# The first block of a two-block network: where the panel casts and low parts stand in the order of ScalarE and VectorE

## The reference

```
proj = rmsnorm(h) @ w_in                      # 4376 columns
hq, hf, hi, hgo, hz, nq, kcm, vcm, ksl, vsl, kwn, vwn, ngate, nz = split(proj)
o_hg = hgrn2_chunkwise(hq, log_f(hf), k(hf), hi)      # gated linear recurrence, 4 heads
y_hg = rmsnorm(o_hg) * sigmoid(hgo) * silu(hz)
kc, vc = compress(kcm), compress(vcm)         # overlapping blocks of 32 tokens, MLP with silu
o_cmp = softmax(q . kc) @ vc                  # compressed keys
o_slc, o_win = attention(q, k_sl, v_sl), attention(q, k_wn, v_wn)   # rope on q and k
y_nsa = (g0 * o_cmp + g1 * o_slc + g2 * o_win) * silu(nz)
h = h + concat(y_hg, y_nsa) @ w_out
h = h + sigmoid(rmsnorm(h) @ w_pg) * (p @ w_pp)
```

## Time and profile before

| | |
|---|---|
| median of 3 runs | 1097.96 us |
| the profiled execution: its own time | 1098.19 us |
| its span | 1096.3 us |
| busy TensorE, VectorE, ScalarE | 1030.5, 730.3, 599.5 us |
| granted clock of TensorE, mean | 0.979 |

### The profile page before, as it was taken

One profiled execution on the slowest core, in us unless ns is written; L12 is line 12 of the kernel. 1 busy time (PEld: TensorE's weight loads), 2 busy tenths in 40 slices (PEclk: granted clock), 3 DMA queues, 4 the chain that ended last, 5 costly groups with the idle time before them and its releaser, 6 DMA issues.

```text
span 1096.3 us, 21297 instructions
## 1 busy us (share of the span) xinstructions
PE 1030.5 (94%) x8933; PEld 971.7 (89%) x8933; DVE 730.3 (67%) x1101; ACT 599.5 (55%) x874; POOL 4.9 (0%) x13
## 2 busy tenths in 40 slices
PE   5999789899999888999999999999999999999997
PEld 4998677799996876998999999999888899999997
DVE  6855556578647455689677766666866588667664
ACT  5643565467536455577746654455655466545552
POOL 1000000000000000000000000000000000000000
PEclk8999899999999899999999999999999999999998
DMA  9453622155645321284543655555455245555531
GB/s 289 143 160 90 195 77 78 39 172 175 188 128 170 101 78 39 77 269 136 181 156 117 230 180 173 184 191 182 117 183 164 77 154 193 189 172 178 189 116 39
DMA packets 144747, 163.57 MB, mean 149 GB/s; under 512 B 6072, under 2 KB 135552, under 8 KB 144672
## 3 DMA queue, kind: packets, MB, share of 16 engines
q1 hardware_dynamic: 143752, 161.04, 45.9%
q10 hardware_dynamic: 632, 1.30, 0.3%
q0 software_dynamic: 288, 0.14, 0.1%
HBM read 161.43 MB, written 1.05 MB: 148 GB/s over the span
## 4 chain that ended last, share of the span: by engine, by line
PE 70%; DVE 12%; ACT 9%; issue 4%; DMA 3%; SPq 0%; ACTq 0%; DVEq 0%
PE ps L441 21%; PE ps L442 21%; PE ps L443 20%; ACT panels_high L1193 4%; DVE panels_low L1735 4%; DMA panels<-in_w_in 3%; ACT probs L1179 2%; PE ps L459 2%; DVE neg_max L1758 1%; DVE squares L1699 1%; DVE probs L1774 1%; DVE input_low L1695 1%; PE ps L664 1%; PE ps L543 1%; PE ps L599 0%
## 5 line engine op out<-in xcount | busy, mean ns | idle before, releaser
L1735 DVE TENSOR_TENSOR panels_low<-panels,panels_high 128x2048 fp32r<-128x2048 f32 (+1 forms) x146 | 330.0, 2263 | 227.8 <-ACT panels_high L1193 227.0
L441 PE MATMUL ps<-input_high,panels_low 128*128 128x256 f32 x1600 | 462.3, 289 | 17.6 <-DVE input_low L1730 7.5
L442 PE MATMUL ps<-input_low,panels_high 128*128 128x256 f32 x1600 | 454.7, 284 | 0.0
L443 PE MATMUL ps<-input_high,panels_high 128*128 128x256 f32 x1600 | 454.4, 284 | 0.0
L1193 ACT CAST panels_high<-panels 128x2048 fp32r<-128x2048 f32 (+1 forms) x146 | 274.3, 1880 | 151.9 <-PE ps L443 122.4
L441 PEld LDWEIGHTS ps<-input_high,panels_low 128*128 128x128 f32 x1600 | 308.8, 193 | 25.5 <-issue 8.1
L442 PEld LDWEIGHTS ps<-input_low,panels_high 128*128 128x128 f32 x1600 | 309.1, 193 | 0.1
L443 PEld LDWEIGHTS ps<-input_high,panels_high 128*128 128x128 f32 x1600 | 308.9, 193 | 0.0
L441 PE MATMUL ps<-ffn_hidden_high,panels_low 128*128 128x256 f32 x352 | 99.2, 282 | 3.1 <-issue 2.9
L442 PE MATMUL ps<-ffn_hidden_low,panels_high 128*128 128x256 f32 x352 | 99.6, 283 | 0.0
L443 PE MATMUL ps<-ffn_hidden_high,panels_high 128*128 128x256 f32 x352 | 99.4, 282 | 0.0
(11 more groups left out here) (288 smaller groups left out, 1309.3 us busy)
## 6 DMA issues: line engine op xcount, KB each, us to landing
panels<-in_ffn_up SPq DMA_DIRECT2D x44, 1024.0 KB, 5.1
panels<-in_w_in SPq DMA_DIRECT2D x32, 1024.0 KB, 6.0
panels<-in_ffn_down SPq DMA_DIRECT2D x22, 1024.0 KB, 4.9
panels<-in_mix_w_in SPq DMA_DIRECT2D x20, 1024.0 KB, 5.5
panels<-in_w_out SPq DMA_DIRECT2D x8, 1024.0 KB, 5.1
panels<-in_w_pg SPq DMA_DIRECT2D x8, 1024.0 KB, 5.7
panels<-in_mix_w_out SPq DMA_DIRECT2D x8, 1024.0 KB, 5.1
panels<-in_w_pp SPq DMA_DIRECT2D x2, 1024.0 KB, 4.8
```

The lines of the kernel that those rows point to most:

```text
L441: pe.matmul(dst, w[1], x[0], start=start, stop=False if not kw else True, **kw)
L442: pe.matmul(dst, w[0], x[1], start=False, stop=False if not kw else True, **kw)
L443: return pe.matmul(dst, w[0], x[0], start=False, stop=stop, **kw)
L1735: V.tensor_tensor(low_slots[slot][:, 0:size], raw[n % SLOTS][:, 0:size], high_slots[slot][:, 0:size].bitcast(F32), ALU.subtract).then_inc( ...
```

## The change

Four things move; no computation is added or left out.

- TensorE: level (7,1) is issued ahead of the rotated keys' product, and so ahead of the compressed keys.
- ScalarE: from `hidden_parts` to the copy of qr1 no casts; up to `cmp_kv` casts only of panels ahead of hz1. From the first `scores` to `on` casts only behind turned copies. The load of the table with exp and tanh moves from behind the output norm to behind the copy of hz0. The third quarter of the mixed rows' high part moves from `on` to `mixed`.
- VectorE: from `hidden_parts` to `cmp_kv` no low parts, but hgo1's at the entry of hgo0's copy. From the first `scores` to `on` low parts only behind row maxima. Row maximum 0 stands ahead of the output norm. The third quarter of the mixed rows' low part stands in the second `nsa_gate`.

```diff
@@ -781,6 +781,7 @@
                     todo(("copy", f"qr{j}"))
                 some(1)
                 gate_chunk()
+                some(16)
                 pe.wait_ge(k_rope_ready, l + 1)
                 begin(f"kr_{l}", 4)
                 pe.matmul(ps[4][:, :], ident, UK[:, 0:512], start=True, stop=False)
@@ -791,7 +792,6 @@
                 product(f"kc_{l}", 5, 32, W2[:, 0:P], HID[:, 0:32])
                 product(f"vc_{l}", 3, 64, HIDV[:, :], W2[:, P:P + 64])
                 todo(("cmp_kv",))
-                some(16)
                 gate_chunk()
                 pe.wait_ge(kcsq_ready, l + 1)
                 product(f"kcss_{l}", 5, 32, head_ones, KC[:, 32:64])
@@ -1335,11 +1335,13 @@
                         "vs": VT[:, 0:T], "ct": PCT[:, :], "hgo0": SG[:, 0:512], "hgo1": SG[:, 512:1024],
                         "hz0": HZ[:, 0:512], "hz1": HZ[:, 512:1024], "nz0": NZ[:, 0:512], "nz1": NZ[:, 512:1024]}
                 tanh_dest = {"hz0": FG[:, 0:512], "hz1": FG[:, 512:1024], "nz0": VH[:, 0:512], "nz1": VH[:, 512:1024]}
-                held = False
+                in_units = held = parts_out = kv_in = False
                 for place, step, *arg in agenda[l]:
                     if step == "copy" and arg[0] in tanh_dest:
                         name = f"{arg[0]}_{l}"
                         copy_out(name, dest[arg[0]], bank(name)[:, :])
+                        if arg[0] == "hz0":
+                            nc.scalar.preload_act_table_set(EXP_TANH)
                         drained(act, name)
                         f(tanh_dest[arg[0]], dest[arg[0]], ACT.Tanh, scale=0.5).then_inc(gate_tanh_ready, 1)
                     elif step == "copy":
@@ -1411,7 +1413,6 @@
                     elif step == "o_norm":
                         act.wait_ge(rope_ready, l + 1)
                         head_rinv([f"oss{g}_{l}" for g in range(2)], UK[:, :], P, 1024).then_inc(o_rinv_ready, 1)
-                        nc.scalar.preload_act_table_set(EXP_TANH)
                     elif step == "cmp_softmax":
                         act.wait_ge(cmp_shift_ready, l + 1)
                         f(SC[:, :], SC[:, :], ACT.Exp).then_inc(cmp_exp_ready, 1)
@@ -1425,13 +1426,16 @@
                         f(SG[:, :], SG[:, :], ACT.Tanh, scale=0.5).then_inc(sig_ready, 1)
                     elif step == "mixed":
                         full(act, f"nz1_{l}")
-                        mixed_high(l, None, (0, 1))
+                        mixed_high(l, [f"on0_{l}"], (0, 1, 2))
                     elif step == "on":
-                        mixed_high(l, [f"on{g}_{l}" for g in range(2)], (2, 3))
-
+                        mixed_high(l, [f"on{g}_{l}" for g in range(2)], (3,))
+
+                    in_units = (in_units or step == "scores") and step != "on"
                     held = (held or (step, *arg) == ("copy", "nz1")) and step != "on"
-                    if not held:
-                        split_high(place)
+                    parts_out = (parts_out or step == "hidden_parts") and (step, *arg) != ("copy", "qr1")
+                    kv_in = kv_in or step == "cmp_kv"
+                    if not held and not parts_out and (not in_units or step == "turned"):
+                        split_high(place, len(SPLIT_KEYS) if kv_in else SPLIT_NO[("hz1", l)])
 
                 squares(nidx, lambda g: drained(act, f"wo_{l}_{g}"), lambda g: split_after(f"wo_{l}_{g}") if g < 2 else None)
                 split_after(f"wo_{l}_2")
@@ -1947,6 +1951,7 @@
                 for g in range(2):
                     split_after(f"hq{g}_{l}")
                 split_after(f"hi{NT - 1}_{l}")
+                in_units = parts_out = False
                 for place, kind, *arg in agenda[l]:
                     if kind == "level":
                         level(*arg)
@@ -2015,6 +2020,7 @@
                                                          ALU.mult, ALU.mult)
                         ins.then_inc(kc_ready, 1)
                     elif kind == "o_norm":
+                        row_max(f"n{l}", 0, 8 * l)
                         dve.wait_ge(o_rinv_ready, l + 1)
                         step(V.scalar_tensor_tensor(QP[:, :], QP[:, :], vec("hgrn_onorm_g", l), UK[:, :],
                                                     ALU.mult, ALU.mult))
@@ -2045,7 +2051,7 @@
                                              r2.rearrange("p (n h) -> p n h", n=NT), gates[:, :, 0:8], ALU.mult))
                         V.tensor_tensor(s3, s3, r2.unsqueeze(2).to_broadcast([P, 16, 16]),
                                         ALU.mult).then_inc(cp_ready, 1)
-                    elif kind == "scores":
+                    elif kind == "scores" and arg[0] > 0:
                         row_max(f"n{l}", arg[0], 8 * l + arg[0])
                     elif kind == "normalise":
                         u = arg[0]
@@ -2069,6 +2075,8 @@
                         s = slice(arg[0] * 512, (arg[0] + 1) * 512)
                         dve.wait_ge(gate_tanh_ready, 4 * l + arg[0] + 3)
                         link(V.scalar_tensor_tensor(NZ[:, s], VH[:, s], 1.0, NZ[:, s], ALU.add, ALU.mult))
+                        if arg[0] == 1:
+                            mixed_low(l, 2)
                     elif kind == "mixed":
                         mixed_low(l, 0)
                         mixed_low(l, 1)
@@ -2077,9 +2085,12 @@
                         full(dve, name)
                         V.scalar_tensor_tensor(Y[:, 1536:2048], bank(name)[:, :], 0.5, NZ[:, 512:1024],
                                                ALU.mult, ALU.mult).then_inc(free(name), 1)
-                        mixed_low(l, 2)
                         mixed_low(l, 3)
-                    if kind not in ("level", "k_pad"):
+                    parts_out = (parts_out or kind == "hidden_parts") and kind != "cmp_kv"
+                    in_units = (in_units or kind == "scores") and kind != "on"
+                    if (kind, *arg) == ("copy", "hgo0"):
+                        split_low(place, SPLIT_NO[("hgo1", l)] + 1)
+                    elif kind not in ("level", "k_pad") and not parts_out and (not in_units or kind == "scores"):
                         split_low(place)
 
                 add_out(f"wo_{l}_", "", 2 * l + 1)
```

## The result

The changed kernel takes 1059.38 us (median of 4 runs, 1058.83 to 1059.88) against 1098.03 of the kernel before: ratio 0.965, 95% interval 0.9636 to 0.9663, faster by 38.65 us. The forecast was 1065, the range 1060 to 1075: the sign and the mechanism came out, the time is 5.6 us shorter than the forecast (the gain is 4.8 us above the sum's 33.8, the rest is the rounding up from 1064.4 to 1065), and it lies outside the range.

The account below looks back on a forecast made before the run. TensorE's idles in the two attention stages and the slow clock behind them were taken as the loss. Removing 39.5 us and keeping 5.7 gives 33.8 off 1098.19, 1064.4, forecast as 1065 for thin covers; range 1060 to 1075.

Parts of the forecast that it names:

- the sum's 33.8: Both layers' attention stages: 39.5 us of idle and clock loss removed, 5.7 us kept, gain 33.8 us.
- The gate half behind the compressed keys: Layer 0's gate product after the compressed keys: level (7,1) drained at 117.9, wanted at 119.1, 1.2 us to spare.
- the cast that holds back unit 2's exponentials: ScalarE in the units: the cast of nz1 would delay unit 2's exponentials by 1.1 us.
- the two waits that stay: Before the first output product, 1.6 us, and for unit 6's turned copies, 1.05 us, in each layer.
- the casts: Rival in the units: casts behind turned copies delay exponentials, 10.8 us less gain if all reach TensorE, 1075; chance 0.13.
- given back later: Rival behind the units: panels wo2 to pg1 cast late on the shorter path; all returned, 1098; chance 0.03.
- the sum's clock term: Slow TensorE stretches in both stages: 5.2 us removed in layer 0 and 2.85 in layer 1, none left behind kept idles.
- the idle kept: TensorE waits left in each layer's stage: 0.2+1.6+1.05 = 2.85 us, 5.7 us in both.
- five and two stretches: Half-rate TensorE stretches counted: five in layer 0 costing 5.2 us, two in layer 1 costing 2.85 us.
- the 0.2 us for the cross copy: ScalarE's cross copy ready at 126.0, wanted by the output product at 126.2: thinnest cover, any lack costing one for one.
- everything removed: Bound of the gain: all idle and clock loss in both stages gone, 39.5 us, 1058.7.
- The clock rival: Rival: the clock falls behind two kept idles in each layer, 1.4 us each, 5.6 us in all, 1070; chance 0.10.

Follow-up runs that it names:

- e3: Kernel before plus never-read products on TensorE only while it waits for the hidden values, 7 in layer 0 and 4 in layer 1; 1100.01 us.
- e7: Changed kernel with first two quarters' high parts ahead of nz1's copy and half the first wo1 output rows ahead of unit 6's values product; 1056.04 us.
- e2: Kernel before with only the units' rule: casts behind turned copies, low parts behind row maxima; 1079.97 us.
- e4: Changed kernel with level (7,1) back behind the compressed keys; 1077.22 us.
- e5: Changed kernel with the cast of hz1 early again, behind hgo0's copy and ahead of the key copies; 1059.89 us.
- e9: Changed kernel with row maximum 0, the table load and the mixed rows' third quarter in their old places; 1065.86 us.
- e8: Kernel before plus never-read products on TensorE in four of its idles in each layer; 1093.91 us.
- the remaining moves: Row maximum 0 ahead of the output norm, table load behind hz0's copy, mixed rows' third quarter earlier; alone in the kernel before 1096.16 us.

## Why the prediction was right or wrong

**Right.** The order of all three queues came out as followed. The gate half behind the compressed keys, wanted at 119.1 and found at 119.1 (the trace's 119.41 less its later start of 0.3); the cast that holds back unit 2's exponentials; the two waits that stay, both before the instructions named; no wait before any transpose; clock at 1.00. Of the rivals, the casts reached no transpose, no clock fell in the stage, and nothing became slower; but part of the gain was given back later, 0.7 us behind each stage, which the prediction priced only as all or nothing.

**Wrong: the sum, in two of its terms.** The step that failed is the sum's clock term, and beside it the idle kept. By the landmarks the idle fell by 15.8+15.75-2.2-2.2 = 27.2 us, where the sum had 31.4-5.7 = 25.7; and TensorE's busy time fell by 7.2+4.2 = 11.5 us, where the step on the clock had 5.2+2.85 = 8.1. Together that is 38.7 us for 33.8.

- The clock term was too small by 3.4 us. It priced five and two stretches and left out the compressed keys and level (7,1) between the two idles, 2.13 us at half rate in layer 0 and 1.75 in layer 1, which take 1.0 after. e3 shows what they are: at full clock they gave nothing, for the idle behind them took the time. Summing idles one by one, one must add them; that is 1.1+0.7 us. The other 1.6 us are the way the profile draws a matmul: its end stands about 0.15 us behind the point where the next could start (a gate half of 2.95 us from start to start is drawn as 3.11), and each idle is drawn too short by up to that much, with the rest counted as busy time, in some twelve places. The starts show it: set side by side, the stretch that the kernel before draws as 3.20 us of idle before unit 0's transposes takes 3.36 us more, that of 1.35 us before hz1's product 1.48, the others 0.07 to 0.16 us more than drawn. e7 tests it: it removes 2.13 us of drawn idle, and each stage is 2.45 us shorter.
- What stays was too large by 1.5 us: kept were 1.26 and 0.87 us and nothing before hz1's product, for 1.6, 1.05 and 0.2. The first was likened to layer 1's 1.69 us. Against this, the 0.2 us for the cross copy was not in the sum.
- The range was too narrow at its near end. The prediction itself gave 1058.7 for everything removed, took a value near that end, and still closed the range at 1060. With the clock term as measured, that end would have been at 1055.
- Left out was what is given back: 1.4 us in all. That the whole time fell by 38.65 us, so near to the stages' 38.7, is luck: behind the second stage TensorE ran at half clock for 12.7 us in the profiled execution of the kernel before and for 8.1 us in that of the changed kernel, and that part is 0.6 us shorter although 0.7 us is given back in it. No edit is made there.

A sum by places would have avoided the first: the start of the gate half behind the change against its start before, 6.8 us, holds idle and slow products in one.

**The clock rival and the rule.** The largest idle kept, 1.26 us, brought no slow stretch in either layer of the two traces of the changed kernel, nor in those of e2, e4, e5 and e9, which have it too. Elsewhere one and the same idle cost differently from run to run. That of 1.69 us in layer 1 had no slow stretch behind it in the kernel before, and in e8 the clock was 0.72 over the 6 us behind it. That of 1.84 us between the layers had one in 4 of 13 profiled executions, at 1.5 us each. The Trainium skill (TensorE: Matmul & The Clock Gate, Part 1: The HAM clock gate) says that the gate's window runs free of the kernel, so that the number of slow matmuls varies over runs of the same kernel. The traces agree. So the prediction's zero for the kept idles was not safe: no slow stretch was seen behind 1.26 us, but nothing here shows that none can come.

**Open.** Which of the remaining moves gives back the 0.7 us behind each stage; and why e3 was slower than the kernel before.

## What to carry to other kernels

Where an in-order engine makes weights ready for later and also stands in the chain of the next product, put the former behind the instruction that hands the chain on, and first move whatever it would then delay (here one small level, worth 17.7 us). Price such a move by the start of a landmark product before and after, with the queues followed, and not by adding idles: idle and half-rate time between two waits are one thing. Look behind the last landmark too, for what is given back there. A part that gives 1.3 us alone can be worth 6.4 (4.7 by the order of the queues) once the wait behind it is gone, so an edit measured alone says little about its place in a set.

## What was not expected of the hardware

Filling an idle with useless products kept the clock up (1.00 through 3 us of fillers), but its fall moved to the next idle, of 2.9 us, and with four idles filled only 4.0 of 8.1 us arrived.

The same idle of 1.84 us was followed by full clock in nine profiled executions and by a slow stretch in four. The kernel before ranged from 1094.33 to 1102.6 us over the 41 runs beside the experiments, and the clock carries the upper end: its 8 runs of 1099.48 us and more are those with a mean clock of 0.974 to 0.976, and the other 33 have 0.978 or more and at most 1098.79 us. The landing of a panel, before which ScalarE stands (6.1 us in layer 0 of the profile, 5.0 in e2), moves the start of the compressed keys by as much; in the changed order it does not stand there, and its stages were alike to 0.03 us in two runs.
